# Unread full-array products between the units of a gated scan on TensorE

## What is computed

```
S_t = diag(exp(log_g_t)) S_{t-1} + k_t^T v_t,   o_t = q_t S_t
scores = einsum('bhtk,bhsk,bhtsk->bhts', q, k, decay);  intra = scores @ v
o_l = forward scan + flipped backward scan, latent tokens start from the context's state
```

## Time and profile before

| what | value |
|---|---|
| runs, median (lowest to highest) | 2969.94 us (2968.53 to 2978.02), three runs |
| profiled execution: its time, its span | 2969.85 us, 2968.1 us |
| TensorE matmul busy | 2424.4 us, 82% of the span |
| VectorE busy | 2110.2 us, 71% |
| ScalarE, GpSimd busy | 1124.8 us, 840.8 us |
| mean granted TensorE clock | 0.924 of full speed |
| scan of layer 0, scan of layer 1 | 206 to 344 us, 2039 to 2128 us of the span |

### The profile page before, as it was taken

The page is one execution under the profiler, slowest core; times in us unless marked ns, Lnnn a source line. Parts: engine busy times, 40 slices in busy tenths (PEclk is TensorE's granted clock), DMA queues, the critical chain, the costliest instruction groups (busy, mean ns, idle before and its releaser), DMA issues. The chain is left out here.

```text
span 2968.1 us, 36810 instructions
## 1 busy us (share of the span) xinstructions
PE 2424.4 (82%) x13114; PEld 1822.0 (61%) x13114; DVE 2110.2 (71%) x4654; ACT 1124.8 (38%) x2650; POOL 840.8 (28%) x688
## 2 busy tenths in 40 slices
PE   5979799896659888888888888688797897777776
PEld 3779565674659777777777777478556542223222
DVE  3567763499949888888888888667653898745444
ACT  3433354336633333333333333342344433334332
POOL 1004001230004434343433434103004453433431
PEclk8995799998889999999999999797798999999999
DMA  5210205264379999999999999221103999999997
GB/s 213 89 32 2 96 4 188 77 235 165 142 297 400 419 419 420 420 419 419 419 420 420 418 416 407 101 82 33 39 1 131 420 421 421 421 421 422 422 422 300
DMA packets 147671, 817.13 MB, mean 275 GB/s; under 512 B 16200, under 2 KB 17800, under 8 KB 64672
## 3 DMA queue, kind: packets, MB, share of 16 engines
q0 software_dynamic: 73728, 536.90, 43.7%
q1 hardware_dynamic: 73760, 277.87, 24.2%
HBM read 796.89 MB, written 17.83 MB: 274 GB/s over the span
## 5 line engine op out<-in xcount | busy, mean ns | idle before, releaser
L2412 POOL DMA_INDIRECT pair_ring<-in_uv_first,eid x256 | 395.0, 1543 | 780.9 <-DVE pair_sum L2555 274.5
L2051 PE MATMUL ps<-pair_ring,pair_diag 128*128 128x512 f32 x1024 | 475.4, 609 | 143.5 <-ACT pair_diag L2130 139.4
L2436 PE MATMUL ps<-peer_h,peer_uv 128*128 128x256 f32 x2048 | 474.8, 386 | 40.4 <-DMA peer_uv<-in_uv_dense 40.4
L2262 DVE CUSTOM_DVE_ANT_0 pair_ring<-pair_ring,hT 128x1024 f32<-128x1024 f32 x256 | 312.9, 1222 | 208.7 <-DMA pair_ring<-in_uv_rows,eid 208.6
L2051 PEld LDWEIGHTS ps<-pair_ring,pair_diag 128*128 128x128 f32 x1024 | 187.1, 192 | 421.0 <-ACT pair_diag L2130 222.6
L2436 PEld LDWEIGHTS ps<-peer_h,peer_uv 128*128 128x128 f32 x2048 | 387.3, 194 | 94.2 <-DMA peer_uv<-in_uv_dense 30.6
L119 PE MATMUL ps<-h_both 128*128 128x256 f32 x1024 | 316.0, 309 | 104.4 <-DVE h_both L2592 104.3
L2543 DVE CUSTOM_DVE_ANT_0 pair_ring<-pair_ring,hT 128x1024 f32<-128x1024 f32 x256 | 312.2, 1220 | 121.0 <-DMA pair_ring<-in_uv_first,eid 120.3
L2012 POOL DMA_INDIRECT pair_ring<-in_uv_rows,eid x256 | 270.4, 1056 | 397.9 <-PE ps L2051 360.2
L120 PE MATMUL ps<-h_both 128*128 128x256 f32 x1024 | 299.5, 292 | 0.0
L121 PE MATMUL ps<-h_both 128*128 128x256 f32 x1024 | 298.9, 292 | 0.0
(11 more groups left out here) (439 smaller groups left out, 4738.5 us busy)
## 6 DMA issues: line engine op xcount, KB each, us to landing
peer_uv<-in_uv_dense SPq DMA_DIRECT2D x128, 1024.0 KB
ada_slab<-in_ada_w SPq DMA_DIRECT2D x20, 2048.0 KB, 8.2
proj_slab<-in_w_fm SPq DMA_DIRECT2D x38, 512.0 KB, 3.5
route_slab<-in_w_pq SPq DMA_DIRECT2D x32, 512.0 KB
peer_gates<-dense_stage SPq DMA_DIRECT2D x4, 4096.0 KB, 13.1
peer_gates<-peer_gates SPq DMA_DIRECT2D x16, 1024.0 KB, 21.6
fm<-in_w_out SPq DMA_DIRECT2D x16, 512.0 KB, 4.2
fm<-in_ada_w SPq DMA_DIRECT2D x3, 2048.0 KB, 11.9
```

Of the source, the lines that this page charges most:

```text
L2051: mm = nc.tensor.matmul(ps[:, 4 + 2 * t + half, :], diag[:, s % DG, :], ring[:, s % R, D_MODEL + half * BANK:D_MODEL + (half + 1) * BANK], ...
L2262: nc.vector.tensor_tensor_reduce(out=row, in0=row, in1=hT[:, s // NS], scale=1.0, scalar=0.0, op0=ALU.mult, op1=ALU.add, accum_out=dots[:, ...
L2412: nc.gpsimd.indirect_dma_start(out=ring[:, s % R], out_offset=None, in_=d["uv_first"], in_offset=bass.IndirectOffsetOnAxis(ap=eid[:, s // ...
L2436: mm = nc.tensor.matmul(ps[:, e % 2, 0:n], us[:, e % SW, k, :], hw[:, k, :], start=(k == 0), stop=(k == DC - 1))
```

## The change

A function `dense()` issues one product of the 128x128 identity with the first 512 columns of `xT`, all 128 rows, into bank 7, which nobody reads at that time. It waits for nothing and signals nothing. It is called after each of the seven units of a pair of the GLA group, once more after that pair's diagonal unit (8 calls for a pair, 16 for a layer), and 3*nt + 2 times in a row at the very beginning of TensorE's stream of the scan, ahead of the wait for the first `ready`: 14 times in layer 0, 8 times in layer 1. Nothing else changes, and no other engine's stream does.

```
+                        def dense():
+
+                            nc.tensor.matmul(ps[:, 7, :], ident[:], xT[:, 0, :], start=True, stop=True)
+
                         def scores(pr):
...
                                             if j == 1 and t == TT - 1:
                                                 mm.then_inc(unit_mm, 1)
-
+                                if c == 0:
+                                    dense()
+
+                            if c == 0:
+                                dense()
                             n = EN * pr + 2 * NU
                             bank_free(n)
                             bank_free(n + 1)
...
+                        for _ in range(3 * nt + 2):
+                            dense()
                         for pr in range(4):
                             scores(pr)
```

## The result

| | before | after |
|---|---|---|
| median of the runs | 2969.34 us | 3019.22 us |
| lowest to highest, four runs each | 2968.53 to 2978.02 | 2998.87 to 3037.21 |
| profiled execution, its span | 2969.85, 2968.1 us | 3008.31, 3006.5 us |
| mean granted clock, profiled execution | 0.924 | 0.923 |

The ratio is 1.0161, 95% interval 1.0132 to 1.0189: the change makes the kernel 1.6% slower, and scatters its runs over 38 us. Each run lists its own mean clock: 0.930 at 2998.87, 0.923 at 3008.31, 0.914 at 3030.14 and 0.912 at 3037.21 us.

What follows compares the result with a forecast made beforehand. TensorE at half clock was taken to bound the scan of layer 0 and the same stretch of layer 1. Layer 0 at +2.5 and layer 1 at +5 gave +7.5 us on 2969.85, 2977 us, range 2955 to 3001.

Steps and rivals of the forecast that it cites:

- no change: Whole kernel: time within about 0.3%, 8.9 us, of before, 2961 to 2979 us; 42 in 100.
- The row at the start: Scan begin: products hidden in TensorE's wait at clock 1.00, nothing delayed; then a 2.4 us wait in layer 0.
- I take it that the clock falls right at the start in both layers: Scan begin, both layers: the gap behind the row and the weak 32-row work after it drop the clock to 0.50.
- At the end of a pair it gets denser … I take the rise there: End of the first pair: clock rises to full; layer 0's second pair then gains 6.7 us.
- the prediction's own sum of 3.5: Scan of layer 0: first pair +11.2, second pair -6.7, outputs -1.0 us; taken as +2.5 after VectorE's share.
- the clock never rises in the group: GLA group: all 16 products cost 1.72 us, 27.5 us a layer; 3000 us in one layer, 3019 in both; 20 in 100.
- Price of one: TensorE: one added product costs 0.86 us at clock 1.00 and 1.72 us at 0.50.
- Sum of layer 1: Scan of layer 1: first pair +11.7, second -2.1, outputs -1.8, sum +7.8; taken as +5, ends +3 and +8 us.
- the clock holds: Rival, clock 1.00 from the row on: layer 0 -10, layer 1 -4.5 us, 2955 us; 17 in 100.
- The spread: Runs: if the clock depends on where the pause falls, it may differ between runs and the spread grows from 9.5 us.
- The forecast's own range: Whole kernel: both lower and both upper ends of the two layers' sums, given as 2968 to 2982 us.

Runs made afterwards that it cites:

- e1: Changed kernel with only the products in a row at the scan's begin (14 and 8), none behind units or diagonals: 2970.53 us, ratio 0.9989.
- e3: Changed kernel with all its products in layer 1 and none in layer 0: 2972.57 us, ratio 1.0009, one of ten runs at 3001.71 us.
- e8: Changed kernel with products in layer 0 only, plus two more behind the first pair's diagonal unit: 2984.76 us, ratio 1.0043.
- e4: Changed kernel with two products in place of one at each place behind a unit, the row as it was: 2998.03 us, ratio 1.0075.
- e11: Changed kernel without a row in either layer, products behind units and diagonals in layer 1 only: 3002.51 us, ratio 1.0096.
- e2: Changed kernel with all its products in layer 0 and none in layer 1: 3005.10 us, ratio 1.0104.
- e5: The kernel without a pause: changed kernel, products in layer 0 only, row of 17, one more product behind the first pair's third unit: 2961.00 us, ratio 0.9965.
- e9: Changed kernel with products in layer 0 only and a row of 17, no extra product behind the third unit: 2998.95 us, ratio 1.0086.
- e7: Changed kernel with each product cut to 64 of the 128 rows, same 512 columns: 3049.23 us, one execution.

## Why the prediction was wrong

Predicted were 2977 us, 2955 to 3001, with 42 in 100 for no change; it was 3019 us. The reading of the bound held: TensorE at half clock. The step that failed is the rise of the clock at the end of the first pair.

- **The row at the start** costs nothing: right, shown by the row alone (ratio 0.9989). Its 28 records ran at 1.00 and the pause behind it was 2.19 us, forecast 2.4.
- **"I take it that the clock falls right at the start in both layers"**: right for layer 0 (it fell at 219.5 us), wrong for layer 1 in the profiled execution. The two pauses are 2.19 and 1.94 us. Behind the one comes a unit of 3.1 us (most of it at 0.50 already), behind the other one of 1.0 us and a product. The trace of the row alone (e1) has the same pause of 1.95 us in layer 1 with no products behind the units, and there the clock falls at 2049.9 us, 3.4 us behind the pause: so the products behind the units count. Whether layer 0 fell for its longer unit or for its pause, a quarter of a microsecond longer, wasn't separated. Layer 1 seems to lose it at times too: e3's one run in ten.
- **"At the end of a pair it gets denser … I take the rise there"**: wrong, and this is the miss. The clock stayed at 0.50 through both pairs. It was an argument from two neighbours (a stretch of narrow products that didn't raise the clock, 2 us of outputs that did), and the new work lay between them. One product before and one behind the diagonal didn't do it; two more did (e8). That term was to give back 2.6 + 6.7 + 1.0 us in layer 0, and without it the second pair costs its full 8 products, 13.8 us, as well: 24.1 us in all. With the dearer products of the next point, 16 x 0.48 = 7.7 us, the prediction's own sum of 3.5 becomes 35.3 us, and 35.0 were measured. It is the rival "the clock never rises in the group", which had 20 in 100, in layer 0. That this rival's time for both layers, 3019 us, is also the measured median is chance: the median lies between runs of 3008 and 3030 us, and by the measured prices both layers lost give some 68 us more than before, 3037 us.
- **Price of one**: too low. At 0.50 it is 5.61 - 3.41 = 2.20 us instead of 1.72; 16 of them give 35.2 us, and the scan grew by 35.0. The rival's 27.5 us, some 25 at the end, was short by the same. At 1.00 the step of the kernel without a pause is 222.33 - 219.35 = 2.98 us against half of 3.41, 1.27 us instead of 0.86. The price was read where products of one shape stand in a row. Between 32-row products each one has two changes of shape, and the surplus hangs on them: a second product right behind the first costs 1.72 and 0.86 us (e4), the unit between products grows from 3.41 to 3.61 us, and a lone product takes 2.00 and 1.05 us. By this working a change costs about 0.2 us at either clock; what happens in it no trace shows.
- **Sum of layer 1**: forecast +5, measured -0.5. Its clock held, so this was the rival "the clock holds" (-4.5) in one layer; the dearer product, 16 x 0.4 us, is more than the 4 us between the two. Where the clock is lost it costs +33.4 (e11), not the 24 that the rival for both layers had for it (3019 - 2969.85 - 25).
- **The spread**: the last sentence of the prediction said that runs may differ by where the pause falls, and they did. Layer 0 lost and layer 1 held is 3008.31 us. With 33 us for a lost clock in layer 1 the two longest runs, 3030 and 3037 us at mean clocks of 0.914 and 0.912, would be those where layer 1 lost it, for all or part of the group. This is inferred from e3, e11 and the mean clocks; no trace of those two runs was taken. By it layer 1 lost the clock twice in four runs of the changed kernel and once in ten of e3; why more often is open. Nor is there a trace of the shortest run, 2998.87 us at 0.930, which stays unexplained.
- **"The clock holds from the row on"**, -10 us in layer 0: the kernel without a pause shows -9.5. The number was right and its reason wasn't. The prediction took 13 us as TensorE's gain and VectorE as the limit that leaves 10 of them. In that kernel TensorE is busy in 51.98 of the 52.21 us between its first unit and its first output, and VectorE still waits 8.6 us for it, in seven waits: TensorE is the limit, and the dearer product takes some 6.5 us (16 x 0.41) of its gain.
- **The forecast's own range** was added up wrong: both lower ends, 0 and +3, give 2973 us, not 2968. It changes nothing in the outcome.

## What to carry to other kernels

Work that is added to hold a clock pays only if it holds it without a break; at the low clock one product cost 2.20 us instead of 1.27 and nothing was paid back. So close the waits first, to less than 0.6 us (here 17 products instead of 14, and one where the banks run full), look at the granted clock by stretches, and time several runs: an arrangement at the edge may show itself in their spread. Where the clock is lost already, three dense products together brought it back within 5.4 us (e8), where sixteen strewn in singly never did (e2). And a price that is read from products of one shape in a row was too low here for one that stands between others.

## What the hardware showed unexpectedly

- Keeping and regaining differ: one product of 512 columns behind each unit of 32 narrow records held the clock at 1.00 for 52 us (e5), and the same stream at 0.50 didn't raise it in over 90 us (the changed kernel, e2), nor in 77 us (e9).
- A pause of 0.61 us behind such work was enough to lose it (e9), while one of 2.57 us between full-array products wasn't.
- TensorE busy all the time on 64 of 128 rows fell from 1.00 to 0.50 within 2.3 us of its start (e7, 206.6 to 208.9 us).
- A change between 32-row and full-array f32 products costs about 0.2 us at either clock, by the working above (e4, e5, the changed kernel).
- The scan of layer 1, unchanged, got its clock back 49.9 us after its begin in the kernel before and 70.7 us in e2, and took 89.8 and 93.1 us.
- The free row, which changes the length of neither scan, came with a narrower spread: 2969.22 to 2972.90 us in ten runs, 2968.48 to 2979.48 in twenty of the kernel before. No experiment here explains that.
